# Last expert round written out of the loop, weight units rounded and split in halves

## The reference

```python
def expert_block(args):
    xb, e = args
    return (jax.nn.silu(xb @ w_gate[e]) * (xb @ w_up[e])) @ w_down[e]
...
y = yb.reshape(P, D)[dest] * g_sorted[:, None].astype(t.dtype)
out = jax.ops.segment_sum(y, tok_sorted, num_segments=N)
...
return rms_norm(x, g_final)
```

## Time and profile before

| what | before |
|---|---|
| median of three runs | 1509.11 us (1508.2 to 1510.22) |
| the profiled execution, its own time | 1508.2 us |
| its span, first to last instruction | 1506.6 us |
| PE busy | 1473.8 us (98%), 7046 matmuls and 7046 weight loads |
| DVE busy | 1190.4 us (79%) |
| ACT busy | 984.9 us (65%) |
| POOL busy | 124.3 us (8%) |
| DMA moved | 462.54 MB, mean 307 GB/s |
| mean granted TensorE clock | 0.995 of full speed |

### The profile page before, as it was taken

The page is one execution under the profiler, slowest core; times in us unless marked ns, Lnnn a source line. Parts: engine busy times, 40 slices in busy tenths (PEclk is TensorE's granted clock), DMA queues, the critical chain, the costliest instruction groups (busy, mean ns, idle before and its releaser), DMA issues.

```text
span 1506.6 us, 19532 instructions
## 1 busy us (share of the span) xinstructions
PE 1473.8 (98%) x7046; PEld 1218.5 (81%) x7046; DVE 1190.4 (79%) x1069; ACT 984.9 (65%) x866; POOL 124.3 (8%) x131
## 2 busy tenths in 40 slices
PE   6999999999999999999999999999999999999996
PEld 5767888888989888888888888888888888888884
DVE  7665544454785778988988988988898898898898
ACT  6555344434523577777777777777777777777775
POOL 0000300000442084000000000000000000002000
PEclk9999999999999999999999999999999999999998
DMA  9413897554632569999999999999999999999993
GB/s 340 164 57 118 290 413 253 190 173 140 200 135 85 168 234 392 407 382 387 389 365 387 381 366 389 395 357 386 399 354 383 395 362 378 392 373 375 388 408 127
DMA packets 200200, 462.54 MB, mean 307 GB/s; under 512 B 9000, under 2 KB 18272, under 8 KB 200160
## 3 DMA queue, kind: packets, MB, share of 16 engines
q1 hardware_dynamic: 191632, 436.26, 79.2%
q0 software_dynamic: 6912, 25.17, 4.2%
q10 hardware_dynamic: 1616, 0.56, 0.1%
HBM read 442.04 MB, written 19.92 MB: 307 GB/s over the span
## 4 chain that ended last, share of the span: by engine, by line
PE 92%; DVE 1%; ACT 1%; issue 1%; DVEq 0%; ACTq 0%
PE bank L1407 29%; PE bank L1409 28%; PE bank L1408 28%; PE bank L1574 2%; PE bank L1684 1%; PE bank L1423 0%; PE bank L1812 0%; DVE X L1367 0%; PE bank L1541 0%; PE bank L1765 0%; PE bank L1549 0%; ACT w_hi L544 0%; PE bank L1713 0%; PE bank L1778 0%; PE bank L1692 0%
## 5 line engine op out<-in xcount | busy, mean ns | idle before, releaser
L857 DVE TENSOR_TENSOR w_lo<-raw,w_hi 128x2048 fp32r<-128x2048 f32 x414 | 947.6, 2295 | 227.8 <-ACT w_hi L544 227.2
L544 ACT ACTIVATE w_hi<-raw 128x2048 fp32r<-128x2048 f32 x414 | 793.8, 1920 | 441.0 <-PE bank L1409 438.7
L1407 PE MATMUL bank<-w_hi,t_hi 128*128 128x512 f32 x1312 | 514.6, 392 | 5.4 <-DVE w_lo L857 3.6
L1409 PE MATMUL bank<-w_hi,t_lo 128*128 128x512 f32 x1312 | 509.7, 388 | 0.0
L1408 PE MATMUL bank<-w_lo,t_hi 128*128 128x512 f32 x1312 | 509.4, 388 | 0.0
L1407 PEld LDWEIGHTS bank<-w_hi,t_hi 128*128 128x128 f32 x1312 | 246.8, 188 | 59.5 <-issue 7.4
L1409 PEld LDWEIGHTS bank<-w_hi,t_lo 128*128 128x128 f32 x1312 | 246.6, 188 | 51.4
L1408 PEld LDWEIGHTS bank<-w_lo,t_hi 128*128 128x128 f32 x1312 | 246.9, 188 | 50.0 <-issue 0.7
L1407 PE MATMUL bank<-w_hi,h_hi 128*128 128x512 f32 x576 | 231.2, 401 | 0.0
L1409 PE MATMUL bank<-w_hi,h_lo 128*128 128x512 f32 x576 | 225.2, 391 | 0.0
L1408 PE MATMUL bank<-w_lo,h_hi 128*128 128x512 f32 x576 | 224.5, 390 | 0.0
(11 more groups left out here) (272 smaller groups left out, 822.0 us busy)
## 6 DMA issues: line engine op xcount, KB each, us to landing
raw<-in_w_gate_moe_dram SPq DMA_DIRECT2D x114, 1024.0 KB, 8.2
raw<-in_w_up_moe_dram SPq DMA_DIRECT2D x113, 1024.0 KB, 8.4
raw<-in_w_down_moe_dram SPq DMA_DIRECT2D x112, 1024.0 KB, 7.5
raw<-in_w_in_rec_dram SPq DMA_DIRECT2D x16, 1024.0 KB, 5.5
raw<-in_w_gate_dense_dram SPq DMA_DIRECT2D x14, 1024.0 KB, 5.4
raw<-in_w_up_dense_dram SPq DMA_DIRECT2D x14, 1024.0 KB, 5.2
raw<-in_w_down_dense_dram SPq DMA_DIRECT2D x14, 1024.0 KB, 4.8
raw<-in_w_in_attn_dram SPq DMA_DIRECT2D x9, 1024.0 KB, 13.7
```

Of the source, the lines that this page charges most:

```text
L544: act.activation(w_hi[:, (u - 1) % SPL, :], raw[:, r, :], ACT.Copy).then_inc(hi_done, 1)
L857: dve.tensor_tensor(w_lo[:, s, :], raw[:, r, :], w_hi[:, s, :].bitcast(F32), ALU.subtract).then_inc(lo_done, 1)
L1407: pe.matmul(o, lh, rh, start=start, stop=False)
L1409: return pe.matmul(o, ll, rh, start=False, stop=stop)
```

## The change

1. **Units in halves.** ACT rounds a unit in two instructions of 1024 columns; the first raises the new `hi_half`, the second `hi_done`. DVE subtracts in two, waits for each, and raises `lo_half` and `lo_done`. PE waits for `lo_half` at the start of a unit and for `lo_done` (`unit_rest`) before the first matmul that reads the second half.
2. **The last round apart.** The loops run `before` = rounds - 1 times, and the body, now a function `expert(last)`, follows once more with `last=True`. That copy has no row transposes and no `gather_hi` and `gather_lo`, splits no units ahead, and SP does not load them; POOL's last row fetch is gone. PE transposes `SL` behind the block b = 2, ACT copies `ST` at b = 3, and DVE adds the pieces of `back` to X at b = 3 to 6, one in each.
3. **The end.** The last unit finishes bank YB first (`y_half`), then YB+1. The product goes to hi and lo parts (free columns of `t_hi` and `t_lo`) in place of `ybuf`, `ST` is float32r, and the scatter is hi and lo matmuls. ACT squares halves of tiles, DVE turns the first half's sum into the bias of the root, and output is scaled and stored in halves.

```diff
-        ST = sb("ST", [P, TOK])
+        ST = sb("ST", [P, TOK], F32R)
...
+        y_hi = [t_hi[:, 4 * m:4 * m + 4, CAP:2 * CAP] for m in range(2)]
+        y_lo = [t_lo[:, 4 * m:4 * m + 4, CAP:2 * CAP] for m in range(2)]
...
-            for u in range(AHEAD):
-                load(expert_unit(u, 0), U0 + FFN_UNITS + u)
-
             ov = out[0].rearrange("(t p) d -> p t d", p=P)
             for t in range(TT):
-                sp.wait_ge(out_done, t + 1)
-                sp.dma_start(ov[:, t, :], outb[:, t, :]).then_inc(stored, 16)
-            sp.wait_ge(stored, 16 * TT)
+                for m in range(2):
+                    sp.wait_ge(out_done, 2 * t + m + 1)
+                    ms = slice(m * BLK, (m + 1) * BLK)
+                    sp.dma_start(ov[:, t, ms], outb[:, t, ms]).then_inc(stored, 16)
+            sp.wait_ge(stored, 16 * TT * 2)
...
-            pool.wait_ge(unit_done, before * FFN_UNITS + (U0 + 4 * FB + 1 - FFN_UNITS))
-            pool.dma_start(xrow, sent_v[:, bass.ds(before + 1, 1), :]).then_inc(row_block, 16)
...
-                    act.activation(w_hi[:, (u - 1) % SPL, :], raw[:, r, :], ACT.Copy).then_inc(hi_done, 1)
+                    for half, signal in ((slice(0, UNIT // 2), hi_half), (slice(UNIT // 2, UNIT), hi_done)):
+                        act.activation(w_hi[:, (u - 1) % SPL, half], raw[:, r, half], ACT.Copy).then_inc(signal, 1)
...
+                    if last and b == 3:
+                        wait_full(TR)
+                        act.activation(ST[:], bank[TR][:, 0:TOK], ACT.Copy).then_inc(free[TR], 1)
...
+            act.wait_ge(y_half, 1)
+            act.activation(y_hi[0], bank[YB][:].rearrange("p (c n) -> p c n", c=4), ACT.Copy).then_inc(yh_done, 1)
+            act.wait_ge(unit_done, unit_at(U0 + FFN_UNITS))
+            act.activation(y_hi[1], bank[YB + 1][:].rearrange("p (c n) -> p c n", c=4), ACT.Copy).then_inc(yh_done, 1)
+            saw_product(YB, YB + 1)
+
+            def part_square(t, m):
+                saw(LAST[t][m])
+                drained(LAST[t][m])
+                ms = slice(m * BLK, (m + 1) * BLK)
+                act.activation(U[:, t, ms], X[:, t, ms], ACT.Square,
+                               accum_out=ss[:, 4, 2 * m + t:2 * m + t + 1]).then_inc(part_sq, 1)
+
+            part_square(0, 0)
+            part_square(1, 0)
             for t in range(TT):
-                saw(*LAST[t])
-                drained(*LAST[t])
-                link(act.activation(U[:, t, :], X[:, t, :], ACT.Square, accum_out=ss[:, 4, t:t + 1]))
-                act.activation(ss[:, 4, 2 + t:3 + t], ss[:, 4, t:t + 1], ACT.Sqrt, scale=1.0 / D,
-                               bias=epsc[:, 0:1]).then_inc(sq_done, 1)
+                part_square(t, 1)
+                act.wait_ge(part_sq, 3 + t)
+                act.wait_ge(bias_set, t + 1)
+                act.activation(ss[:, 4, 4 + t:5 + t], ss[:, 4, 2 + t:3 + t], ACT.Sqrt, scale=1.0 / D,
+                               bias=ss[:, 4, 6 + t:7 + t]).then_inc(sq_done, 1)
...
-                    dve.wait_ge(hi_done, n.step("unit"))
+                    n.step("unit")
                     s, r = (u - 1) % SPL, (u - 1) % RAW
-                    dve.tensor_tensor(w_lo[:, s, :], raw[:, r, :], w_hi[:, s, :].bitcast(F32),
-                                      ALU.subtract).then_inc(lo_done, 1)
+                    for half, ready, signal in ((slice(0, UNIT // 2), hi_half, lo_half),
+                                                (slice(UNIT // 2, UNIT), hi_done, lo_done)):
+                        dve.wait_ge(ready, n.at("unit"))
+                        dve.tensor_tensor(w_lo[:, s, half], raw[:, r, half], w_hi[:, s, half].bitcast(F32),
+                                          ALU.subtract).then_inc(signal, 1)
...
+                    if last and b == 3:
+                        saw(TR)
+                        dve.wait_ge(y_back, 16 * 2 * TT)
+                    if last and b > 2:
+                        r, t = (b - 3) // 2, (b - 3) % 2
+                        link(dve.scalar_tensor_tensor(X[:, t, :], back[t][r], row_f[:, 3, t, r:r + 1], X[:, t, :],
+                                                      ALU.mult, ALU.add))
...
+            dve.wait_ge(last_done, TT + 1)
+            saw_product(YB, YB + 1)
+            for m in range(2):
+                dve.wait_ge(yh_done, m + 1)
+                dve.tensor_tensor(y_lo[m], bank[YB + m][:].rearrange("p (c n) -> p c n", c=4), y_hi[m].bitcast(F32),
+                                  ALU.subtract).then_inc(free[YB + m], 1)
+            for m in range(2):
                 for t in range(TT):
-                    dve.scalar_tensor_tensor(X[:, t, :], back[t][r], row_f[:, 3, t, r:r + 1], X[:, t, :], ALU.mult,
-                                             ALU.add).then_inc(dve_seq, 1)
-                n.step("seq", 2)
-                dve.wait_ge(dve_seq, n.at("seq"))
+                    b = LAST[t][m]
+                    wait_full(b)
+                    xb = X[:, t, m * BLK:(m + 1) * BLK]
+                    dve.scalar_tensor_tensor(xb, bank[b][:], gl[:, t:t + 1], xb, ALU.mult,
+                                             ALU.add).then_inc(free[b], 1)
             for t in range(TT):
-                scatter_add(t, LAST[t])
+                dve.wait_ge(part_sq, t + 1)
+                dve.tensor_scalar(ss[:, 4, 6 + t:7 + t], ss[:, 4, t:t + 1], 1.0 / D, EPS, ALU.mult,
+                                  ALU.add).then_inc(bias_set, 1)
...
-                pe.wait_ge(lo_done, n.step("unit"))
+                pe.wait_ge(lo_half, n.step("unit"))
                 return s
+
+            def unit_rest():
+
+                pe.wait_ge(lo_done, n.at("unit"))
...
+                    if k == per // 2:
+                        unit_rest()
...
+                    if split_end and u == per // 2 - 1:
+                        for m in range(2):
+                            for c in range(2):
+                                if m < c:
+                                    unit_rest()
+                                hs = slice((u * 2 + c) * P, (u * 2 + c + 1) * P)
+                                ws = slice(c * D + m * BLK, c * D + (m + 1) * BLK)
+                                last = triple(bank[ybanks[m]][:], h_hi[:, g % 2, hs], h_lo[:, g % 2, hs],
+                                              w_hi[:, s, ws], w_lo[:, s, ws], False, c == 1)
+                            last.then_inc((y_half, unit_done)[m], 1)
+                        continue
...
+                    if last and b == 2:
+                        pe.wait_ge(last_done, TT)
+                        open_bank(TR)
+                        for t in range(TT):
+                            one_hot = pe.transpose(bank[TR][:, t * P:(t + 1) * P], SL[:, t, :], ident[:])
+                        one_hot.then_inc(full[TR], 1)
...
+            expert(True)
+            for m in range(2):
+                pe.wait_ge(yh_done, m + 1)
+                for t in range(TT):
+                    open_bank(LAST[t][m])
+                    pe.matmul(bank[LAST[t][m]][:].rearrange("p (c n) -> p c n", c=4), ST[:, t * P:(t + 1) * P],
+                              y_hi[m], start=True, stop=False)
+                drained(YB + m)
+                for t in range(TT):
+                    pe.matmul(bank[LAST[t][m]][:].rearrange("p (c n) -> p c n", c=4), ST[:, t * P:(t + 1) * P],
+                              y_lo[m], start=False, stop=True).then_inc(full[LAST[t][m]], 1)
```

More of the change, by code:

```diff
@@ L794, in _ @@
                     hidden_hi(g)
-                split_to(U0 + FFN_UNITS + AHEAD)
+                split_to(U0 + FFN_UNITS + (0 if last else AHEAD))
+            with act.Fori(0, before) as i:
+                n.enter(i, dict(ROUND, **{f"loaded{r}": 16 * FFN_UNITS // RAW for r in range(RAW)}, stored=16))
+                expert(False)
                 act.wait_ge(y_stored, n.step("stored", 16))
@@ L1813, in row_transposes, with expert @@
                     last.then_inc(full[b], 1)
[L1815 to L1819 removed]
             gather()
             pe.wait_ge(rounds_in, 1)
[L1824 to L1826 removed]
+            before = pe.value_load(nrounds[0:1, 1:2], min_val=NE - 1, max_val=2 * NE - 1)
+            def expert(last):
                 for b in range(FB):
```

80 lines of the change are left out of this document (39 added, 41 removed).

## The result

| | before | after |
|---|---|---|
| median of four runs, alternating on one chip | 1509.22 us (1508.2 to 1510.22) | 1495.26 us (1494.55 to 1496.17) |
| the profiled execution, its span | 1508.2, 1506.6 us | 1494.55, 1492.4 us |

What follows compares the result with a forecast made beforehand. PE's pace sets the routed stage, so only its waits can be won: 2.2 + 1.6 + 0.5 + 0.6 + 8.4 = 13.3 us off 1508.2 gives 1494.9, plus 0.9 for the median: 1495.8 us; range 1493.0 to 1501.0.

Steps and rivals of the forecast that it cites:

- Late units: In the routed rounds, PE's waits for late weight units go with halves: -2.2 us, bounds 0 to -2.6.
- The first unit: At the start, PE gets the first half-unit 1.9 us earlier: -1.6 us, range 0 to -2.1, capped at the rotated heads.
- In the recurrence: PE's 0.51 us wait for a DVE product behind a weight unit shrinks: -0.5 us, range 0 to -0.6.
- The last round: On PE, eight row transposes go (0.9 us) and two transposes of `SL` come in (about 0.3): -0.6 us.
- The additions' cover: Last round: DVE's four `back` additions cost nothing, covered by its 1.9 us lead from halves; without it, 1.0 us.
- The end: Behind PE's last product, 10.6 us remain against 19.1: -8.4 us taken, bounds -7.0 to -9.3.
- The chain: Steps behind the last product: scatter 2.3 us, additions 4.3, last root 6.0, last scaling 8.1, end 10.6.
- Steady rounds cost nothing: In routed rounds, halves add 2 to 3 us to DVE and 4 to ACT, hidden by their slack.
- The slower rival: ACT's and DVE's grown loop bodies no longer fit and are fetched anew on seven passes: 43 us, 1539 us; 4%.

Runs made afterwards that it cites:

- halves_only: The kernel before with every weight unit rounded and split in halves, rounds in one loop and the end as before: 1503.07 us, ratio to before 0.9966.
- whole_1: The changed kernel with only the first weight unit whole: 1499.32 us, ratio to the kernel before 0.9938.
- whole_66: The changed kernel with only the 66th weight unit whole: 1493.59 us, ratio to the kernel before 0.99.
- last_only: The changed kernel with every weight unit whole, last round and end staying as changed: 1501.71 us, ratio to the kernel before 0.9955.

## Why the prediction was right, and where not

- **Late units, -2.2 forecast: -2.7.** A round is 118.47 us for 118.86, 0.39 less, times seven, without a weight wait left. The seventh is the last round, 0.36 shorter in halves_only. The places were right. The late unit was taken too small: in the round that begins at 893.19 before and at 890.18 after, PE is 0.30 us ahead by its first hidden transposes (65.59 us in for 65.29), where 0.25 was assumed, and the wait behind the row transposes gives the 0.06 that were assumed.
- **The first unit, -1.6: -1.54 at the rotated heads.** The size is right by luck of the route. The working had the clock at 0.50 behind the first product; in the profile it stayed at 1.00, PE won more, and the heads capped it, at a lower mark than the 2.1 estimated. In whole_1 the lack of this half came with 2.98 us, more than that, with the products slow for long.
- **In the recurrence, -0.5: +0.5.** This is the one step that failed. "With halves DVE starts 1.91 - 1.06 = 0.85 earlier" held (the 0.89 us of idle are gone). What the step left out is the unit ahead of it, whose halves take 4.92 us beside POOL for 3.54 whole. It takes turns with POOL (last section). whole_66 undoes just that, and the wait is gone: from the heads to the second round it is 0.75 us shorter than before.
- **The last round, -0.6: -0.5**, with halves. The additions' cover was named rightly: without the halves it is gone, and last_only loses 0.9 us between H and T. By the lengths of the last round 1.3 us need both parts. Against that, halves shorten the old end by 0.8 us and the new one not at all. By the ratios the parts are worth 5.1 and 6.8 us, 11.9 for 13.6 of the whole, and by the pieces 12.4 for 13.0; the intervals of the ratios are as wide as the difference.
- **The end, -8.4: -8.7** (19.1 to 10.4). The chain came as added up, within 0.5 us at each link. The experiments add how it is shared: with the three units ahead put back, 5.5 us return, of which 0.4 to 0.8 are the clock's, which falls while PE waits, and up to 0.66 the table load's. The other edits gave 3.2 us with the units there, and three of them only 0.7 without.
- **Steady rounds cost nothing:** DVE and ACT have 22 and 29 us more work and PE waits for neither.
- **The slower rival** (loops fetched anew, 1539 us) is out: it needed 1.9 us on each pass to decide, and the rounds are 0.39 shorter. The instruction queues' bytes alone would not settle it for ACT's and DVE's loops, since the page names no engine for them.

The sum was 1.6 up to H, 3.3 from there to T and 8.4 behind it, 13.3 us. The pieces of the profile give 1.5, 2.8 and 8.7, which is 13.0, and the medians 13.96, with runs of after 1.6 us apart. Between H and T the recurrence is off by 1.0 us and the rounds made up half of it; the total is closer than its terms.

## What to carry to other kernels

Split an operation in halves where its successor waits, not everywhere: one unit of 411, beside another engine's work, cost 1.3 us of the gain, and for the units without a waiting successor no profile shows a gain. Two operations of one engine beside two of another that take turns with it are held up twice. Look at each handover that a faster start reaches, since a wait removed there comes back at the next link until the slowest chain between is shorter. Where TensorE waits for others at the end, take work off those others first, and don't read the cost of its products off rows at a lowered clock.

## What the runs showed of the hardware that was not expected

- DVE and POOL beside each other: one subtraction of 2048 columns takes DVE 2.29 us alone and 3.54 beside two additions of POOL's (5.03 us); as two of 1024 it takes 2.36 alone and 4.92 beside them (3.95). Which of the two gives way depends on how the work is cut. Single instructions, of after and then of before (timelines):

```profile
422.38 2.47 DVE L884 TENSOR_TENSOR w_lo<-raw,w_hi 128x1024 fp32r<-128x1024 f32 x1
...
423.73 2.49 POOL L427 TENSOR_TENSOR work<-work 128x512 f32<-128x512 f32 x1
```
```profile
426.24 3.56 POOL L424 TENSOR_TENSOR work<-work 128x512 f32<-128x512 f32 x1
```

In after the instructions end in turn: POOL's first addition at 423.78 (422.27 and 1.51 us), DVE's first half at 424.85, POOL's second at 426.22, DVE's second half at 427.30. A turn of DVE's is 1.1 us and one of POOL's 1.4. In before POOL's first ends at 426.28, DVE's whole unit at 428.42 and POOL's second at 429.80: DVE waits for one turn of POOL's and POOL's second addition for all of the unit. By these ends the two engines take turns here, a whole instruction at a time, and the cut puts a second turn of POOL's, 1.4 us, into the unit; that is the 1.38 us by which it is longer. Why they exclude each other, no run here shows.
- TensorE slowed after waits, but not in every profile: at the start in eight of the fourteen (by the distance of its products; the granted clock shows it in five), in the attention in two, in the recurrence in one. Runs of one kernel spread by 1.2 to 5.4 us, which is as much as most edits here are worth.
- The last stores took 2.5 to 3.5 us from the last scaling to the end of the span, with the same stores.
